# First mixer: two value copies on VectorE, a later order of weight splits, and one modulation product behind the second rank's norm

## The reference, cut to what matters

```python
mod = (c_act @ mod_w[i] + mod_b[i]).reshape(B, 6, D)[:, :, None, :]
hin = x * (1.0 + mod[:, 1]) + mod[:, 0]
...
def mla_mixer(h, cos, sin, w_in, q_norm, w_uq, kv_norm, w_ukv, w_o):
    proj = h @ w_in
    c_q = rms_norm(proj[..., :MLA_Q_RANK], q_norm)
    c_kv = rms_norm(proj[..., MLA_Q_RANK:MLA_Q_RANK + MLA_KV_RANK], kv_norm)
    k_rope = apply_rope(proj[..., MLA_Q_RANK + MLA_KV_RANK:], cos, sin)
    q = (c_q @ w_uq).reshape(B, S, H, DN + DR).transpose(0, 2, 1, 3)
    q = jnp.concatenate([q[..., :DN], apply_rope(q[..., DN:], cos[:, None], sin[:, None])], -1)
    kv = (c_kv @ w_ukv).reshape(B, S, H, DN + DV).transpose(0, 2, 1, 3)
    k = jnp.concatenate([kv[..., :DN], jnp.broadcast_to(k_rope[:, None], (B, H, S, DR))], -1)
    v = kv[..., DN:]
    o = causal_softmax_attention(q, k, v, (DN + DR) ** -0.5)
    return merge_heads(o) @ w_o
```

## Time and profile before

| | |
|---|---|
| median of 3 runs | 907.64 us (906.79 to 909.63) |
| the profiled execution: its own time | 908.5 us |
| its span, first to last instruction | 906.7 us |
| mean granted TensorE clock | 0.985 |
| PE busy | 851.8 us, 94% of the span |
| DVE busy | 719.2 us, 79% |
| ACT busy | 507.0 us, 56% |
| chain that ended last, by engine | PE 57%, DVE 20%, ACT 10%, DMA 7%, issue 5% |

### The profile page before, as it was taken

The page is one execution under the profiler, slowest core; times in us unless marked ns, Lnnn a source line. Parts: engine busy times, 40 slices in busy tenths (PEclk is TensorE's granted clock), DMA queues, the critical chain, the costliest instruction groups (busy, mean ns, idle before and its releaser), DMA issues.

```text
span 906.7 us, 14872 instructions
## 1 busy us (share of the span) xinstructions
PE 851.8 (94%) x5722; PEld 774.9 (85%) x5722; DVE 719.2 (79%) x1138; ACT 507.0 (56%) x877; POOL 76.7 (8%) x121
## 2 busy tenths in 40 slices
PE   3899899999999999999999999999899999999976
PEld 3767689999999989999798889999779899889964
DVE  4776888878878878889888788686778766789996
ACT  2226657455345465568473445544475768756992
POOL 2110100010000000132000022010000000000000
PEclk9999899999999999999999999999999999999998
DMA  9997774788887748986847789987535784446621
GB/s 319 366 314 268 255 253 142 234 279 284 304 317 276 258 161 293 381 323 201 310 164 253 275 249 284 273 238 248 180 118 164 244 278 164 136 156 224 217 93 47
DMA packets 124998, 216.31 MB, mean 239 GB/s; under 512 B 12507, under 2 KB 98247, under 8 KB 118784
## 3 DMA queue, kind: packets, MB, share of 16 engines
q1 hardware_dynamic: 108156, 133.48, 44.4%
q0 software_dynamic: 13808, 73.51, 23.3%
q10 hardware_dynamic: 2964, 8.37, 2.7%
HBM read 214.18 MB, written 1.15 MB: 237 GB/s over the span
## 4 chain that ended last, share of the span: by engine, by line
PE 57%; DVE 20%; ACT 10%; DMA 7%; issue 5%; SPq 0%; POOL 0%; DVEq 0%; ACTq 0%
PE bank L586 9%; PE bank L588 9%; PE bank L587 9%; PE bank L592 6%; PE bank L594 6%; PE bank L593 6%; DVE w_lo L1759 5%; DMA modraw<-in_mod_w 4%; DVE modsum L1791 3%; ACT w_hi L1199 2%; DVE of L1791 2%; PE bank L691 2%; DMA vv<-in_mod_w 1%; ACT kk L1261 1%; DMA raw<-in_moba_w_in 1%
## 5 line engine op out<-in xcount | busy, mean ns | idle before, releaser
L1759 DVE TENSOR_TENSOR w_lo<-raw,w_hi 128x1024 fp32r<-128x1024 f32 (+1 forms) x236 | 276.1, 1205 | 65.5 <-ACT w_hi L1199 64.9
L586 PE MATMUL bank<-h_hi,w_hi 128*128 128x256 f32 x1072 | 306.5, 286 | 5.3 <-DVE w_lo L1759 4.0
L588 PE MATMUL bank<-h_hi,w_lo 128*128 128x256 f32 x1072 | 303.2, 283 | 0.0
L587 PE MATMUL bank<-h_lo,w_hi 128*128 128x256 f32 x1072 | 303.2, 283 | 0.0
L1199 ACT ACTIVATE w_hi<-raw 128x1024 fp32r<-128x1024 f32 (+1 forms) x236 | 237.4, 1038 | 65.7 <-DMA raw<-in_moba_w_in 20.1
L586 PEld LDWEIGHTS bank<-h_hi,w_hi 128*128 128x128 f32 x1072 | 205.5, 192 | 7.9 <-issue 5.2
L587 PEld LDWEIGHTS bank<-h_lo,w_hi 128*128 128x128 f32 x1072 | 205.6, 192 | 1.3 <-issue 0.5
L588 PEld LDWEIGHTS bank<-h_hi,w_lo 128*128 128x128 f32 x1072 | 205.5, 192 | 0.0
L592 PE MATMUL bank<-w_hi,o_hi 128*128 128x512 f32 x304 | 122.4, 403 | 6.7 <-ACT w_hi L1199 3.3
L594 PE MATMUL bank<-w_hi,o_lo 128*128 128x512 f32 x304 | 119.3, 392 | 0.0
L593 PE MATMUL bank<-w_lo,o_hi 128*128 128x512 f32 x304 | 119.0, 392 | 0.0
(11 more groups left out here) (322 smaller groups left out, 1261.6 us busy)
## 6 DMA issues: line engine op xcount, KB each, us to landing
raw<-in_ffn_w_in SPq DMA_DIRECT2D x88, 512.0 KB, 6.6
modraw<-in_mod_w POOLq DMA_DIRECT2D x32, 1024.0 KB, 6.9
raw<-in_ffn_w_out SPq DMA_DIRECT2D x44, 512.0 KB, 7.6
modraw<-in_ada_w POOLq DMA_DIRECT2D x16, 1024.0 KB, 5.4
raw<-in_attn_w_in SPq DMA_DIRECT2D x26, 512.0 KB, 5.4
raw<-in_moba_w_in SPq DMA_DIRECT2D x24, 512.0 KB, 9.3
modraw<-in_mod_w POOLq DMA_DIRECT2D x20, 512.0 KB, 4.6
modraw<-in_ada_w POOLq DMA_DIRECT2D x16, 512.0 KB, 4.8
```

What stands on the lines that cost most here:

```text
L586: pe.matmul(dst, cut(hi(u)), a_hi, start=first, stop=False, skip_group_check=True)
L587: pe.matmul(dst, cut(hi(u)), a_lo, start=False, stop=False, skip_group_check=True)
L588: return pe.matmul(dst, cut(lo(u)), a_hi, start=False, stop=last, skip_group_check=True)
L1759: dve.tensor_tensor(lo(v), raw_unit(v), hi(v).bitcast(F32), ALU.subtract).then_inc(sem("w_lo_ready"), 1)
```

## The change

Four edits, all in the first mixer:

1. DVE no longer runs a `modulate(1)` between the two `rank_normed` calls; it stands behind the rotary key. On PE the spread of the rotary key stands ahead of `rank_sum(1)`.
2. The values of heads 4 to 7 (banks 6 and 7) are copied to `vv` by DVE in step 2; before, ACT's `values_out(1)` did it in step 2. PE waits for the new semaphore `late_values`.
3. ACT's numbers for steps -1 to 8 are 0, 2, 2, 2, 3, 4, 5, 6, 7, 9; before 0 to 9.
4. DVE's numbers are -1, 0, 1, 1, 2, 3, 4, 5, 6, 7; before -1 to 8.

```diff
         beside_units = {
-            "mla": {t: split0 + t + 1 - AHEAD for t in range(-1, 9)},
+            "mla": {t: split0 + u - AHEAD for t, u in enumerate((0, 2, 2, 2, 3, 4, 5, 6, 7, 9), -1)},
...
             rank_sum(0)
             mla_unit(5, bank[1], 1)
-            rank_sum(1)
             pe.wait_ge(sem("fold_summed"), 2)
...
             ins.then_inc(sem("kr_spread"), 1)
+            rank_sum(1)
             pe.wait_ge(sem("c_full"), 2)
...
                 if h == 4 and t == 0:
-                    pe.wait_ge(sem("ukv_copied"), 8)
+                    pe.wait_ge(sem("late_values"), 2)
...
                 if t == 3:
-                    pe.wait_ge(sem("ukv_copied"), 8)
+                    pe.wait_ge(sem("ukv_copied"), 6)
+                    pe.wait_ge(sem("late_values"), 2)
                     fold(1, (4, 5, 6, 7))
...
                     keys_out(1)
-                if t == 2:
-                    values_out(1)
...
                     beside(t)
-                    if t in units:
+                    if kind == "mla" and t in lows:
+                        ahead(split0 + lows[t])
+                    elif t in units:
                         ahead(units[t] + AHEAD - 1)
...
             modulate(1)
             rank_normed(0)
-            modulate(1)
             rank_normed(1)
...
                 sem("kr_ready"), 1)
+            modulate(1)
+
             def rotate(j):
...
+            lows = dict(enumerate((-1, 0, 1, 1, 2, 3, 4, 5, 6, 7), -1))
+
             def mla_beside(t):
                 if t == 1:
                     rotate(1)
+                if t == 2:
+                    dve.wait_ge(sem("w_used"), unit0("ukv", 1) + 2)
+                    for i, b in enumerate((6, 7)):
+                        at = (i * 12 + 4) * P
+                        dve.tensor_copy(vv[:, at:at + 4 * P], bank[b][:, :]).then_inc(sem("late_values"), 1)
```

## The result

The changed kernel took a median of 901.97 us over 6 executions (897.0 to 906.03); beside it on the same chip the kernel before took 907.76 us (904.49 to 909.63). The ratio is 0.9939, with a 95% interval of 0.9915 to 0.9963. By the medians that is 5.8 us faster, against a forecast of 3.0 us and a range that ended at 902.4.

The account below looks back on a forecast made before the run. It saw a first-mixer chain passing between DVE, PE and ACT, no engine full from 77 to 96 us. Terms 1.5 + 1.9 + 0.8 - 1.2 = 3.0 us gave 904.6 against the median of 907.64; range 902.4 to 908.3.

Parts of the forecast that it names:

- the clock at the fold: PE at `fold(1)`: the fall to 1.2 GHz comes later and for a shorter time; 0.8 us won.
- the first term: Second rank's norm, edit 1: `ukv` 1.8 us earlier, less block 12's delay; 1.5 us won at the first exponential.
- the other two: Edits 2 to 4 in steps 0 to 2, 1.9 us won; extra split behind the attention, 1.2 us lost.
- block 12 behind it: DVE ahead of `rotate(0)`: block 12 lands 6.5 us after its later issue, cutting 1.8 us to 1.6.
- edits 2 to 4, to the fold: DVE and ACT, steps 0 to 2: two waits of 1.07 us go, wholly and about 0.9; 1.9 us won.
- unit 8 behind the attention: Units 8 and 9 both left for `out_projection`: one more DVE split ahead of group 2's fold; 1.2 us lost.
- rival (a): At the fold the clock stays up: 4.2 us won, 903.4 us; chance 0.19.
- a DVE wait on `modraw` of 2.2 us ahead of block 12, not 4: Sign to check in DVE's trace: how long DVE waits for block 12 after its later issue.
- Rival (b): Block 12 lands later, at 71.7 after 8.5 us: 0.9 us won in all, 906.7 us; chance 0.17.
- Rival (d): DVE is the bound with unchanged work; only the 1.5 and the 1.2 count: 907.3 us; chance 0.07.
- Rival (c): Block 12 takes 10.8 us: 1.4 us lost, 909.0 us; slower from a landing 9.4 us after issue; chance 0.11.
- The third term: DVE behind the attention: units 8 and 9 both left, one more split ahead of group 2's fold; 1.2 us lost.

Follow-up runs that it names:

- `rotate(0)` first: Changed kernel with `rotate(0)` ahead of blocks 12 and 13 on DVE; mean 901.1 us, ratio to before 0.9922.
- filled: Among the variants: changed kernel with 12 unneeded PE transposes in its wait ahead of the fold of group 1; mean 901.9 us, ratio to before 0.993.
- unit 8 earlier: Changed kernel with unit 8 converted and split one step earlier, on ACT and DVE; mean 901.7 us, ratio to before 0.9928.
- ACT copies: Changed kernel with the late values copied by ACT again (edit 2 undone); mean 904.1 us, ratio to before 0.9962.
- the filling: Kernel before with 25 unneeded PE transposes, 16 ahead of the wait for `o_lo` and 9 ahead of group 1; mean 903.3 us, ratio 0.9955.

## Why the prediction was wrong

The side was right, and so were the places. The size was not. The step that failed is the clock at the fold, in its own words "If it falls later and for a shorter time, 0 to 0.9 us is won on top. I take 0.8." In its place the runs showed that the clock mostly does not fall in the changed kernel, which is worth 2.2 us in the mean. That is 1.4 of the 2.8 us by which the forecast fell short; 0.5 more is the first term, 0.1 each the other two, and 0.7 is not located. So the clock is half of what the forecast missed, not most of it, as my theory after the result had it.

| step | forecast | measured |
|---|---|---|
| `ukv` | 1.8 us earlier | 2.2 earlier with an early fall, 3.0 without |
| block 12 behind it | takes 0.2 | 0.0 to 1.8 |
| edits 2 to 4, to the fold | 1.9 | 2.0 |
| clock at the fold | 0.8 | 2.2 |
| unit 8 behind the attention | -1.2 | -1.1 |

**The clock.** Before: 7.24 us from the fold to the row unit in the mean of six; changed order of steps: 5.09 in the mean of eight; the difference is 2.2 us, where the forecast had 0.8. The price of a fall was nearly right: 2.0 us to the row unit in the forecast (5.4 for 3.4, with 2.6 on PE alone), 2.4 measured. The odds were not. I had one fall in one trace of before, summed the two idle times (3.3 us before, 2.3 after by my sum; 3.4 and 1.7 in the traces) and gave the clock's staying up 0.19 as rival (a). It stayed up in 7 of 8, counting the changed kernel's variants (1 of 2 in the changed kernel itself). Idle times were summed as if only their total counted, though in one execution the clock fell ahead of the second wait. And a price that is paid (1.6 to 2.9 us) or not at all went into the sum as 0.8, a value between the two outcomes. In the execution profiled with the result the 0.8 was even met, with the clock down for a shorter time: 6.57 us from fold to row unit for 7.41. That was luck; it was the one of eight that fell. Rival (a), with 4.2 us won, had the clock right and was still 1.6 us short of the 5.8. The Trainium skill's page TensorE: Matmul & The Clock Gate, section The HAM clock gate, says that the number of slow products varies between executions of one kernel; the two profiles of the changed kernel agree in that they differ. With the longer waits six of six fell, so there this case shows chance only in how long the clock stayed down (3.4 or 6.8 us), not in whether it fell.

**Edit 1.** The step was right and the size low. Where the clock had fallen early, `ukv` started at 62.1 to 62.8 us without edit 1 (mean 62.54) and 60.0 to 60.6 with it (60.29; the kernel with `rotate(0)` first, at half clock for longer there, is left out); where it had not, at 61.4 to 62.15 (61.67) and 58.5 to 58.9 (58.63). Times of different executions can only be set against each other at like clock ahead of them; a distance avoids this. From `ukv` to the scores it is 13.0 us in before (14.6 to 14.7 in the two profiles where the clock fell in between), 14.77 and 13.72 in the changed kernel, and 13.01 with `rotate(0)` first: that is block 12, and it cost 1.8 and 0.7 us, and 0.0 to 0.4 in three of its variants (filled, unit 8 earlier, ACT copies). The forecast's own mark "a DVE wait on `modraw` of 2.2 us ahead of block 12, not 4" was met on one side by the first profile (3.70) and nearly by the others (2.67, 2.21, 2.37). Where block 12 cost nothing DVE waited 1.96 us for it (edit 1 alone, ACT copies). From its issue it took 6.2 to 7.9 us in these kernels, where I had taken 6.5. Rival (b) was thus half right in the one profile that came with the result. Taken together the first term is about 2.0 us (2.6, midway between the two gains, less 0.6, the mean of the five costs; the profiles are few, and this can be off by half a microsecond), 0.5 above the 1.5 of the forecast.

**Edits 2 to 4.** From the scores to the fold it took 20.76 to 20.79 us in every profile with before's steps, filled or not, and 18.80 to 18.87 in every one with the changed steps and DVE copying. The forecast's 1.9 us, the copies at 1.3 us, and the two removed waits hold. Rival (d), that DVE is the bound, falls. Rival (c) asked for a landing of 9.4 us; none was seen.

**The end.** From the row unit to the dense layer 36.63 us became 37.76 us; moving unit 8 gave 36.62. The third term holds, though its 1.1 us did not show in the mean time of that kernel, whose error is 0.75 us.

**The sum.** 2.0 + 2.0 + 2.2 - 1.1 = 5.1 us against the 5.8 (0.8) measured. The range's lower end does not follow from its own terms either: the clock up and the copies at their lower bound give 903.4 - 0.7 = 902.7, not 902.4. The measured median lies below both.

**What stays open.** For the whole the terms add up; for the parts they don't. By them edit 1 alone should give some 2.6 us (block 12 did not hold up PE in its profile) and gave 0.8 (0.7); edits 2 to 4 alone should give 3.1 and gave 1.6 (0.9); the filling should give 2.4 and gave 4.3 (0.5). For edit 1 alone and for the filling the difference lies behind 140 us, where all of them run the same program: the last column is 768.0 us with edit 1 alone, has a mean of 766.2 in the five executions of before, and of 763.9 in the four of before filled. So of the 4.3 us of the filling only 2.4 are shown at the fold. For edits 2 to 4 it lies elsewhere: their three profiled executions have a mean of 903.3 us and 764.9 in the last column, and what is missing is in the executions above 907 us, of which none was profiled. The last column is longer where more of that stretch ran at 1.2 GHz (correlation 0.7 over all 20), but not by that alone: with 13.6 us of it between 140 and 892 us the kernel before and edit 1 alone took 767.8 and 768.0, and five others 764.8 to 765.7. Whether a fall at the fold makes a later one likelier, whether something else differs there, or six against four executions came out so by chance, these runs don't settle. The forecast's sentence that a shift "should travel through the rest unchanged" holds to 2 or 3 us only: the last column spreads from 762.6 to 768.0 us.

## What to carry to other kernels

Where a wait of PE ends with a lower clock behind it, price that as its own case with its own chance, and get that chance from several executions, not from one trace. A cheap test tells it from work taken off a path: fill the waits with products that nobody reads, and see whether the kernel gets faster and whether the clock stays up in its profile. And where the clock is at stake, the times of a change's parts needn't add up to that of the whole; compare distances between two instructions in traces of several executions.

## What the runs showed of the hardware

Waits of TensorE of 2.05 and 1.37 us, 0.9 us apart (1.16 and 1.1 in one), brought its clock to 1.2 GHz in 6 of 6 executions, in one of them ahead of the second wait; 0.34 to 0.50 and 1.37 us did in 1 of 7, 1.34 and 1.37 us in 0 of 1, and 0.22 and 0.45 us in 0 of 4. The clock was then down for 3.4 us (3 executions) or 6.8 us (4). Twenty-five products of 128x128 that do nothing made the kernel before 4.3 (0.5) us faster, 2.4 of them at the fold. One and the same program of 900 us spread over 9 us (897.0 to 906.03) in six executions.
